# One decoder layer with paged latent attention on TensorE: the sample keys by token move from SyncE's DMA queue to GpSimd's

## The chip, the cores and the metric

The kernel is one program on one core of a Trainium2 chip. The metric is the time of one execution on the device in microseconds (us). The kernel before was run three times: 2036.37, 2043.57 and 2047.83 us, median 2043.57 us.

## What is computed

The reference is one layer of a decoder for two request groups with shared weights: a prompt of 256 tokens, and 8 sample sequences of 8 new tokens each, each behind 1024 cached tokens in 8 pages of 128. Only the part around the change is shown: the attention of one sample sequence over its cached latent (512 wide) and rotary key (64 wide), 16 heads.

```python
c_all = jnp.concatenate([cache_c[pages].reshape(n_past, KV_LORA), cn], axis=0)
kr_all = jnp.concatenate([cache_kr[pages].reshape(n_past, QK_ROPE), krn], axis=0)
q_lat = jnp.einsum('thd,rhd->thr', qn, w_uk)
s = (jnp.einsum('thr,lr->htl', q_lat, c_all) + jnp.einsum('thr,lr->htl', qr, kr_all)) * ATTN_SCALE
p = jax.nn.softmax(jnp.where(mask[None], s, -jnp.inf), axis=-1)
o_lat = jnp.einsum('htl,lr->thr', p, c_all)
return jnp.einsum('thr,rhd->thd', o_lat, w_uv)
```

The latent `c_all` is used twice: in the scores, where it has to lie with the latent index on the partitions ("by latent"), and in the sum over the tokens, where it has to lie with the token on the partitions ("by token").

## The kernel before, in words

All work is written out by hand on five engines, which meet only at semaphores. The weights come as slabs of 1 MB from DRAM into two buffers `w_raw`; ScalarE (ACT) rounds each to `w_hi` and VectorE (DVE) makes the rest `w_lo`, so that TensorE (PE) can multiply in three passes. The stages follow each other: input projections, gates, prompt attention (16 heads, with the products `ukt` for the sample queries between them), the sample stage, output projections, and a feed-forward part of 11 chunks that takes over half of the time. SyncE's queue (SP, SPq in the rows) issues nearly all transfers.

The sample stage is a loop over i = 0..8 in each engine, one sample sequence b per round, with two halves q of four pages each. `w_raw` and `c_raw` have one buffer for each half.

TensorE's round i (L1454 to L1489) is, in this order: `score(i, 0)`; the transposes of the probabilities of sequence i-1 (L1463, L1467); `score(i, 1)`; the scores of the new tokens; `values(i-1, 0)` and `values(i-1, 1)`, 32 matmuls each of `spt` with `c_raw`; and four matmuls with `cnew`. `score(i, q)` waits for `ql_lo_r >= i+1` (L1433), that is for `ql_lo` of sequence i. `values(b, q)` waits for `c_full[q]` (L1446) and raises `c_used` when it is done (L1452).

ScalarE's round i splits the pages of sequence i+1, makes `ql_hi` of sequence i+1 (`query_hi`, L632), and takes the exponentials. VectorE's round i makes `w_lo` of the pages, the maxima and the normed probabilities.

GpSimd (POOL) has one task in this stage: L421 to L424, a loop over b in which it waits for `ql_hi` of b and makes `ql_lo = qlat - ql_hi`.

SyncE loads both forms of the cache. `by_latent(b, q)` (L331) issues four transfers of 288 KB into `t_raw[q]`, which lies over `w_raw`; `by_token(b, q)` (L338) issues four of 256 KB into `c_raw[q]`. Both read the four page numbers from `page_sb` into registers first (`pages_of`, L316 to L320). `by_token(b, q)` waits for `values(b-1, q)` to be done (L341), and `by_token(0, 0)` for the last head of the prompt attention (L343), since `c_raw[0]` lies over buffers of that. In SyncE's loop (L357 to L371) `by_token(i, 0)` and `by_token(i, 1)` stand behind both `by_latent(i+2, q)`, and each of these behind a wait for the `w_lo` of the pages before them (L360); `by_token(0, 1)` stands ahead of the loop (L353).

Of the kernel before, what the change touches and what calls it, by code (L numbers as in the profile page):

```python
# [26 lines left out]
H, DN, DR, DV, R = 16, 128, 64, 128, 512  # L27
RT = R // P
PAST, PAGE = 1024, 128
NPG = PAST // PAGE  # L30
# [20 lines left out]
G0 = {}  # L51
# [6 lines left out]
QUAD = NPG // 2  # L58
# [4 lines left out]
def dense_index(g):  # L63

    return g if g < GS else g - 2 * NB
# [4 lines left out]
def split_index(g):  # L70

    return g - (4 if g > G0["ukt"] else 0) - (4 if g > G0["uv2"] else 0)
# [23 lines left out]
def program(nc, slabs, x, vecs, consts, cache_t, cache, pages, pool_hist, conv_hist,  # L96
            y, kv_out, kr_out, pool_out, conv_out):
    n_phys = cache.shape[0]
# [8 lines left out]
    def sb(name, shape, dt=F32, at=None):  # L107
        n = 4
        for d in shape[1:]:
            n *= d  # L110
        return nc.alloc_sbuf_tensor_at(name, shape, dt, offset=region(n) if at is None else at)

    with ExitStack() as ctx:
        def sem(name):
            return ctx.enter_context(nc.semaphore(name))
# [14 lines left out]
        page_sb = sb("page_sb", [1, NB * NPG], I32)  # L130
# [20 lines left out]
        c_raw = [sb("c_raw0", [P, QUAD * R], at=ch_reg), sb("c_raw1", [P, QUAD * R])]  # L151
# [63 lines left out]
        def const(name, n=None):  # L215
# [8 lines left out]
        vec_in, hist_in, again_in, chist_in = (sem(n) for n in ("vec_in", "hist_in", "again_in", "chist_in"))  # L224
# [3 lines left out]
        slab_used, slab_taken = sem("slab_used"), sem("slab_taken")  # L228
# [9 lines left out]
        sc_done, sc_masked, mx_done, ex_done, rc_done, pn_done, pt_done, pt_taken, pv_done, ohi_done, olo_done = (  # L238
            sem("p_" + n) for n in ("sc_done", "sc_masked", "mx_done", "ex_done", "rc_done", "pn_done", "pt_done",
                                    "pt_taken", "pv_done", "ohi_done", "olo_done"))  # L240
# [4 lines left out]
        c_full, c_used = [sem("c_full0"), sem("c_full1")], sem("c_used")  # L245
# [34 lines left out]
        @block.sync  # L280
        def _(sp):
            def x_part(c):

                sp.dma_start(xT[:, 4 * c:4 * c + 4, :], x[:, 4 * c:4 * c + 4, :]).then_inc(x_in[c], 16)

            def latent_rows(j, n0, n1):

                return (raw[j % 2][:, n0 * 4 * P:n1 * 4 * P].rearrange("p (n c) -> p n c", n=n1 - n0),
                        slabs[n0:n1, :, j * 4 * P:(j + 1) * 4 * P].rearrange("n p c -> p n c"))

            sp.dma_start(vec[:, :], vecs).then_inc(gain_in, 16)
            x_part(0)
            sp.dma_start(*latent_rows(0, 0, 2)).then_inc(slab0_half, 16)
            sp.dma_start(*latent_rows(0, 2, 4)).then_inc(raw_full[0], 16)
            x_part(1)
            sp.dma_start(*latent_rows(1, 0, 4)).then_inc(raw_full[1], 16)
            x_part(2)
            sp.wait_ge(lo_ready, 1)
            sp.dma_start(*latent_rows(2, 0, 4)).then_inc(raw_full[0], 16)
            x_part(3)  # L300
            sp.wait_ge(lo_ready, 2)
            sp.dma_start(*latent_rows(3, 0, 4)).then_inc(raw_full[1], 16)
            sp.dma_start(cst[:, :], consts).then_inc(vec_in, 16)
            sp.dma_start(page_sb[:, :], pages).then_inc(vec_in, 16)
            sp.dma_start(hist[:, :, :], pool_hist).then_inc(hist_in, 16)

            def stream(g0, g1):

                d0 = dense_index(g0)
                with sp.Fori(d0 // 2, (d0 + g1 - g0) // 2) as i:  # L310
                    for s in range(2):
                        sp.wait_ge(lo_ready, i * 2 + (split_index(g0) - d0 + s - 1))
                        sp.dma_start(raw[s], slabs[i * 2 + s]).then_inc(raw_full[s], 16)

            stream(RT, G0["ukt"])
            def pages_of(b, q):  # L316

                first = b * NPG + q * QUAD
                return nc.values_load_multi_w_load_instructions(  # L319
                    page_sb[0:1, first:first + QUAD], engines=(mybir.EngineType.SP,), min_val=0, max_val=n_phys - 1)[1]  # L320

            def whole_slabs(name, free):

                for q in range(2):
                    sp.wait_ge(slab_used, free + q + 1)
                    sp.dma_start(whole[2 + q], slabs[dense_index(G0[name] + 2 + q)]).then_inc(whole_full[q], 16)

            def into_raw(g):
                sp.dma_start(raw[g % 2], slabs[dense_index(g)]).then_inc(raw_full[g % 2], 16)

            def by_latent(b, q):  # L331

                pages4 = pages_of(b, q)
                for j in range(QUAD):
                    sp.dma_start(t_raw[q][:, j * TCOL:(j + 1) * TCOL],  # L335
                                 cache_t[bass.ds(pages4[j], 1)].rearrange("a p c -> (a p) c")).then_inc(t_full[q], 16)

            def by_token(b, q):  # L338

                if b:  # L340
                    sp.wait_ge(c_used, 2 * (b - 1) + q + 1)  # L341
                elif q == 0:
                    sp.wait_ge(pv_done, H)  # L343
                pages4 = pages_of(b, q)
                for j in range(QUAD):
                    sp.dma_start(c_raw[q][:, j * R:(j + 1) * R],  # L346
                                 cache[bass.ds(pages4[j], 1)].rearrange("a p c -> (a p) c")).then_inc(c_full[q], 16)

            for q in range(2):
                sp.wait_ge(lo_ready, G0["ukt"] + q - 1)  # L350
                into_raw(G0["ukt"] + q)
            whole_slabs("ukt", G0["ukt"] - 2)
            by_token(0, 1)  # L353
            for q in range(2):
                sp.wait_ge(slab_used, G0["ukt"] + q + 1)
                by_latent(0, q)
            for i in range(-1, NB):  # L357
                for q in range(2):
                    if i + 2 <= NB:
                        sp.wait_ge(lo_ready, split_index(GS + 2 * (i + 1) + q) + 1)  # L360
                    if i + 2 < NB:
                        by_latent(i + 2, q)
                    elif i + 2 == NB:
                        into_raw(G0["uv2"] + q)
                if i == NB - 1:
                    whole_slabs("uv2", G0["uv2"] - 2)
                if i == -1:
                    by_token(0, 0)
                if i >= 1:
                    for q in range(2):  # L370
                        by_token(i, q)  # L371
            for q in range(2):
                sp.wait_ge(slab_used, G0["uv2"] + q + 1)
                into_raw(G0["attn_out"] + q)
            stream(G0["attn_out"] + 2, NSLAB)
            sp.wait_ge(cs_done, 2 * FT)
            sp.dma_start(conv_out, cstate[:, :, :, :]).then_inc(out_sem, 16)
            for k in range(4):
                sp.wait_ge(y_step, 4 * (k + 1))
                sp.dma_start(y[:, 4 * k:4 * k + 4, :], x1[:, 4 * k:4 * k + 4, :]).then_inc(out_sem, 16)  # L380
            sp.wait_ge(st_done, 16)
            sp.wait_ge(out_sem, 16 * 7)
# [3 lines left out]
        def _(pool):  # L386
# [31 lines left out]
                last.then_inc(qrs_ready, 1)  # L418

            pool.wait_ge(qrs_ready, 4)  # L420
            for b in range(NB):  # L421
                pool.wait_ge(ql_hi_r, b + 1)
                nc.gpsimd.tensor_tensor(ql_lo[:, b % 2, :], qlat[:, b, :, :].rearrange("p j c -> p (j c)"),
                                        ql_hi[:, b % 2, :], ALU.subtract).then_inc(ql_lo_r, 1)  # L424

            pool.wait_ge(chist_in, 16)
            pool.wait_ge(slab_used, G0["ffn"])
# [1245 lines left out]
```

## Time and profile before

| what | value |
|---|---|
| median of three runs | 2043.57 us |
| time of the profiled execution | 2035.44 us |
| span of its trace | 2032.3 us |
| mean granted clock of TensorE | 0.989 |
| busy: TensorE / VectorE / ScalarE / GpSimd | 97% / 54% / 37% / 3% |
| busy in the sample stage, 716 to 839 us of the span (123 us): TensorE / VectorE / ScalarE / GpSimd | 113.96 / 53.74 / 51.95 / 6.33 us |
| DMA engines' mean busy share in that stretch | 0.75, 245 GB/s |

The span is the time from the first to the last instruction of the trace; the execution's own time is 3.1 us more. Busy time is that of instructions that compute: waits, register instructions and DMA issues are not in it. The clock is a share of TensorE's full speed. PEld is the loading of weights into TensorE, which lies beside its matmuls.

### The profile page before, as it was taken

The page shows a single profiled execution, that of the slowest core. Times are in us where ns is not written, and L with a number is a line of the kernel's source. Part 1 is how long each engine was busy: PE and PEld are TensorE (multiplying, and loading weights), DVE is VectorE, ACT ScalarE, POOL GpSimd, SP SyncE. Part 2 cuts the span into 40 slices and gives each one's busy share as a digit, 9 for nine tenths or more (in the row PEclk, how much of TensorE's full clock was granted, in tenths as well). Part 3 has the DMA queues.
Part 4 walks back from the last instruction along what each step waited for, and adds up shares of the span by engine and source line. Part 5 has one row for each costly group of instructions (what it writes and reads, how often), then busy time and mean ns, then how long its engine had stood idle before and what let it go on. Part 6 is the DMA issues. An engine that isn't in the chain of part 4 may idle for free.

```text
span 2032.3 us, 34080 instructions
## 1 busy us (share of the span) xinstructions
PE 1969.3 (97%) x13366; PEld 1942.9 (96%) x13366; DVE 1093.5 (54%) x1472; ACT 754.1 (37%) x813; POOL 54.4 (3%) x196
## 2 busy tenths in 40 slices
PE   8999999999999799999999999999999999999996
PEld 7999999999998688999999999999999999999996
DVE  6864344334345555255556555655556565565657
ACT  5456542332245554133334333333333333333332
POOL 0001000000000000000000000000000000000000
PEclk9999999999999899999999999999999999999998
DMA  6444444444453378544444434434444344443442
GB/s 243 145 145 161 153 145 147 158 150 145 144 186 111 114 248 267 204 162 150 145 146 151 164 140 152 147 142 165 142 147 148 143 164 144 144 152 141 161 145 101
DMA packets 59575, 318.14 MB, mean 157 GB/s; under 512 B 6466, under 2 KB 6658, under 8 KB 26882
## 3 DMA queue, kind: packets, MB, share of 16 engines
q1 hardware_dynamic: 58866, 313.15, 43.7%
q10 hardware_dynamic: 656, 4.27, 0.5%
q8 instruction: 34, 0.56, 0.1%
q14 instruction: 19, 0.16, 0.0%
HBM read 313.08 MB, written 4.32 MB: 156 GB/s over the span
## 4 chain that ended last, share of the span: by engine, by line
PE 90%; DVE 3%; ACT 3%; DMA 2%; issue 1%; SPq 1%; POOL 0%; DVEq 0%; ACTq 0%; POOLq 0%
PE ps L1199 90%; DVE w_lo L753 1%; ACT w_hi L457 1%; DMA c_raw<-in_cache 1%; DMA w_raw<-in_slabs 1%; DVE x L1192 0%; DVE k_rope L753 0%; ACT sm L639 0%; SPq L319 0%; SPq L335 0%; DMA xT<-in_x 0%; DVE neg_max L1029 0%; ACT k_rope L457 0%; SPq L346 0%; DMA w_raw<-in_cache_t 0%
## 5 line engine op out<-in xcount | busy, mean ns | idle before, releaser
L753 DVE TENSOR_TENSOR w_lo<-w_raw,w_hi 128x2048 fp32r<-128x2048 f32 (+1 forms) x267 | 609.7, 2284 | 459.8 <-ACT w_hi L457 459.6
L1199 PE MATMUL ps<-h_hi,w_hi 128*128 128x320 f32 x2512 | 742.2, 308 | 14.6 <-ACT w_hi L457 11.1
L457 ACT ACTIVATE w_hi<-w_raw 128x2048 fp32r<-128x2048 f32 (+1 forms) x267 | 508.3, 1905 | 639.6 <-PE ps L1199 632.8
L1199 PE MATMUL ps<-h_lo,w_hi 128*128 128x320 f32 x2512 | 741.1, 309 | 0.0
L1199 PEld LDWEIGHTS ps<-h_hi,w_hi 128*128 128x128 f32 x2512 | 473.3, 188 | 15.4 <-ACT w_hi L457 11.3
L1199 PEld LDWEIGHTS ps<-h_lo,w_hi 128*128 128x128 f32 x2512 | 471.5, 188 | 0.2
L1199 PE MATMUL ps<-h_hi,w_lo 128*128 128x320 f32 x2512 | 393.6, 308 | 0.0
L1199 PEld LDWEIGHTS ps<-h_hi,w_lo 128*128 128x128 f32 x2512 | 374.9, 187 | 0.0
L1199 PE MATMUL ps<-hid_hi,w_hi 128*128 128x320 f32 x704 | 216.7, 308 | 0.0
L1199 PE MATMUL ps<-hid_lo,w_hi 128*128 128x320 f32 x704 | 216.5, 308 | 0.0
L1199 PE MATMUL ps<-hid_hi,w_lo 128*128 128x320 f32 x704 | 216.5, 308 | 0.0
L1199 PEld LDWEIGHTS ps<-hid_hi,w_hi 128*128 128x128 f32 x704 | 131.9, 187 | 0.5 <-issue 0.3
L1199 PEld LDWEIGHTS ps<-hid_hi,w_lo 128*128 128x128 f32 x704 | 131.9, 187 | 0.0
L1199 PEld LDWEIGHTS ps<-hid_lo,w_hi 128*128 128x128 f32 x704 | 131.9, 187 | 0.0
L753 DVE TENSOR_TENSOR x<-ps,x 128x320 f32<-128x320 f32 x176 | 79.9, 485 | 46.5 <-PE ps L1199 46.4
L740 ACT ACTIVATE silu<-cv,vec 128x336 f32<-128x336 f32 x44 | 25.4, 577 | 213.2 <-DVE cv L1181 213.2
L1199 PE MATMUL ps<-o_hi,w_hi 128*128 128x320 f32 x256 | 75.5, 309 | 1.7 <-ACT w_hi L457 1.7
L1199 PE MATMUL ps<-m_hi,w_hi 128*128 128x320 f32 x256 | 75.3, 308 | 0.0
L1199 PE MATMUL ps<-o_lo,w_hi 128*128 128x320 f32 x256 | 75.3, 307 | 0.0
L1199 PE MATMUL ps<-m_lo,w_hi 128*128 128x320 f32 x256 | 75.3, 307 | 0.0
L1199 PE MATMUL ps<-spt,c_raw 128*128 128x128 f32 x512 | 62.3, 285 | 8.0 <-DMA c_raw<-in_cache 8.0
L1199 PEld LDWEIGHTS ps<-spt,c_raw 128*128 128x128 f32 x512 | 61.0, 201 | 8.5 <-issue 8.4
(212 smaller groups left out, 1749.0 us busy)
## 6 DMA issues: line engine op xcount, KB each, us to landing
w_raw<-in_slabs SPq DMA_DIRECT2D x253, 1024.0 KB, 4.8
w_raw<-in_cache_t SPq DMA_DIRECT2D x64, 288.0 KB, 3.6
c_raw<-in_cache SPq DMA_DIRECT2D x64, 256.0 KB, 3.7
w_whole<-in_slabs SPq DMA_DIRECT2D x4, 1024.0 KB, 6.5
xT<-in_x SPq DMA_DIRECT2D x4, 640.0 KB, 7.5
x_again<-in_x ACTq DMA_DIRECT2D x1, 2560.0 KB, 12.6
out_y<-x SPq DMA_DIRECT2D x4, 640.0 KB, 2.9
w_raw<-in_slabs SPq DMA_DIRECT2D x2, 512.0 KB, 6.1
```

Source lines behind the costliest of these rows:

```text
L457: return nc.scalar.activation(out, in_, ACT.Copy)
L740: nc.scalar.activation(silu[:, f % 2, CW - 1:], cv[:, 2, CW - 1:], ACT.Silu, bias=vec[:, bass.ds(c * FPC + (VEC["conv_b"] + f), 1)]).then_ ...
L753: return nc.vector.tensor_tensor(out, a, b, op)
L1199: return nc.tensor.matmul(out, a, b, start=start, stop=stop, **kw)
```

## The change

The transfers by token leave SyncE's program and are issued by GpSimd. `by_token` is defined there: it reads its four page numbers into GpSimd's registers, then waits, then issues four transfers. `by_token(0, 1)` and `by_token(0, 0)` stand ahead of GpSimd's loop over b, and `by_token(b, 0)` and `by_token(b, 1)` behind the `ql_lo` of b in that loop, for b = 1 to 7. The first waits for the slabs ahead of `ukt` to be used, in place of its old position in SyncE's order. The transfers, their sizes, their buffers and all other waits are the same.

```diff
@@ SyncE
-            def by_token(b, q):
-
-                if b:
-                    sp.wait_ge(c_used, 2 * (b - 1) + q + 1)
-                elif q == 0:
-                    sp.wait_ge(pv_done, H)
-                pages4 = pages_of(b, q)
-                for j in range(QUAD):
-                    sp.dma_start(c_raw[q][:, j * R:(j + 1) * R],
-                                 cache[bass.ds(pages4[j], 1)].rearrange("a p c -> (a p) c")).then_inc(c_full[q], 16)
-
...
-            by_token(0, 1)
...
-                if i == -1:
-                    by_token(0, 0)
-                if i >= 1:
-                    for q in range(2):
-                        by_token(i, q)
@@ GpSimd
             pool.wait_ge(qrs_ready, 4)
+            def by_token(b, q):
+
+                first = b * NPG + q * QUAD
+                pages4 = nc.values_load_multi_w_load_instructions(
+                    page_sb[0:1, first:first + QUAD], engines=(mybir.EngineType.Pool,), min_val=0, max_val=n_phys - 1)[1]
+                if b:
+                    pool.wait_ge(c_used, 2 * (b - 1) + q + 1)
+                elif q == 0:
+                    pool.wait_ge(pv_done, H)
+                else:
+                    pool.wait_ge(slab_used, G0["ukt"])
+                for j in range(QUAD):
+                    pool.dma_start(c_raw[q][:, j * R:(j + 1) * R],
+                                   cache[bass.ds(pages4[j], 1)].rearrange("a p c -> (a p) c")).then_inc(c_full[q], 16)
+
+            pool.wait_ge(vec_in, 32)
+            by_token(0, 1)
+            by_token(0, 0)
             for b in range(NB):
                 pool.wait_ge(ql_hi_r, b + 1)
                 nc.gpsimd.tensor_tensor(ql_lo[:, b % 2, :], qlat[:, b, :, :].rearrange("p j c -> p (j c)"),
                                         ql_hi[:, b % 2, :], ALU.subtract).then_inc(ql_lo_r, 1)
+                if b:
+                    for q in range(2):
+                        by_token(b, q)
```

## Rows read from the trace of the kernel before

**Rows 1.** The page: busy time of each engine, and the chain that ended last.

```profile
PE 1969.3 (97%) x13366; PEld 1942.9 (96%) x13366; DVE 1093.5 (54%) x1472; ACT 754.1 (37%) x813; POOL 54.4 (3%) x196
PE 90%; DVE 3%; ACT 3%; DMA 2%; issue 1%; SPq 1%; POOL 0%; DVEq 0%; ACTq 0%; POOLq 0%
```

**Rows 2.** Who waited for whom, TensorE, 600 to 860 us: total, times, longest.

```profile
PE ps L1199 <- DMA c_raw<-in_cache: 8.0, 4, 2.5
PE ps L1199 <- POOL ql_lo L423: 6.3, 2, 3.8
```

**Rows 3.** Timeline, rounds 3 and 4: start, duration, engine, what, [idle before it].

```profile
744.00 7.41 PE L1199 MATMUL ps<-spt,c_raw 128*128 128x128 f32 x64
...
745.69 0.62 ACT L457 ACTIVATE ql_hi<-qlat 128x512 fp32r<-128x512 f32 x1
...
746.38 1.26 POOL L423 TENSOR_TENSOR ql_lo<-qlat,ql_hi 128x512 fp32r<-128x512 f32 x1 [17.41 <-ACT ql_hi L457]
...
749.13 2.29 DVE L753 TENSOR_TENSOR w_lo<-w_raw,w_hi 128x2048 fp32r<-128x2048 f32 x1
...
751.25 1.06 PE L1199 MATMUL ps<-spt,cnew 128*128 128x128 f32 x8
...
751.73 0.79 DVE L1074 TENSOR_SCALAR s_probs<-s_probs,sample_sum 128x1088 f32<-128x1088 f32 x1
...
752.06 0.48 PE L1199 MATMUL ps<-w_hi,ql_hi 128*128 128x512 f32 x1
...
756.40 5.32 SPq L346 DMA_DIRECT2D c_raw<-in_cache  x8
...
762.46 7.38 PE L1199 MATMUL ps<-spt,c_raw 128*128 128x128 f32 x64 [1.57 <-DMA c_raw<-in_cache]
```

**Rows 4.** Timeline of TensorE: the other rounds that waited, and one that did not.

```profile
727.15 7.38 PE L1199 MATMUL ps<-spt,c_raw 128*128 128x128 f32 x64 [1.81 <-DMA c_raw<-in_cache]
...
798.00 8.97 PE L1199 MATMUL ps<-spt,c_raw 128*128 128x128 f32 x64 [2.06 <-DMA c_raw<-in_cache]
...
816.24 7.39 PE L1199 MATMUL ps<-spt,c_raw 128*128 128x128 f32 x64
...
828.03 9.01 PE L1199 MATMUL ps<-spt,c_raw 128*128 128x128 f32 x64 [2.52 <-DMA c_raw<-in_cache]
```

**Rows 5.** SyncE's issues: line L346 (min/median/max ns), its landing, timeline, chain.

```profile
L346 SPq DMA_DIRECT2D c_raw<-in_cache x56: 332/333/1560, 721.0 to 827.8; - x56
DMA to landing us min/median/max: 2.7/3.7/5.3
614.76 1.90 SPq L346 DMA_DIRECT2D c_raw<-in_cache  x4
716.09 0.30 SPq L319
...
717.60 0.33 SPq L335
```

**Rows 6.** Timelines of TensorE and GpSimd: from the prompt attention into the sample stage.

```profile
682.04 1.66 PE L1199 MATMUL ps<-pt,vv 128*128 128x256 f32 x8
684.78 1.26 POOL L423 TENSOR_TENSOR ql_lo<-qlat,ql_hi 128x512 fp32r<-128x512 f32 x1 [495.09 <-ACT ql_hi L457]
686.19 0.47 PE L1199 MATMUL ps<-w_hi,ql_hi 128*128 128x512 f32 x1 [2.49 <-POOL ql_lo L423]
689.07 0.39 PE L1199 MATMUL ps<-k_rope,q_rope_hi 128*128 128x512 f32 x1
```

**Rows 7.** The same passes one round later, and that stretch's granted clock (last but two).

```profile
697.75 0.77 PE L1199 MATMUL ps<-w_hi,ql_hi 128*128 128x512 f32 x1 [3.77 <-POOL ql_lo L423]
702.71 0.39 PE L1199 MATMUL ps<-k_rope,q_rope_hi 128*128 128x512 f32 x1
698.00:702.00 4.00, 4.00 (x10) 3.17 (x11) 3.86 (x6) 1.25 (x4) 0.00 (x0) 0.50 0.87 272
```

## The prediction

> **What bounds the kernel now.** I read the page first. TensorE is busy for 97% of the span and makes 90% of the chain that ended last; GpSimd is busy for 3% [rows 1]. So whatever makes TensorE stand still is paid in full, and an engine at 3% matters only where TensorE waits for it. Next I asked who waited for whom on TensorE in the sample stage. Two entries touch the change: four waits for the transfers into `c_raw`, 8.0 us together, and two for GpSimd's `ql_lo`, 6.3 us [rows 2]. The first is what the change can win; the second says that `ql_lo` is already on the path where it is late. Last I read the timeline of two rounds, for the order of events and the slack of each [rows 3].
>
> The round, with t = 0 where `values(b-1, 0)` starts (744.00): both halves of the values take 7.25, to 751.25, so one takes 3.6; `cnew` follows and the next `score(b+1, 0)` starts at 752.06, t = 8.1. `ql_hi` of b+1 is ready at t = 2.3 and `ql_lo` of b+1 runs from 2.4 to 3.6. The score that needs it starts at 8.1, so `ql_lo` now has 4.4 us of slack [rows 3]. SyncE issues the eight transfers by token only from 756.40, t = 12.4, though `c_raw` is free at 3.6 and 7.3: that is why TensorE waits 1.57 us at 762.46 [rows 3]. Rounds 2, 6 and 8 wait 1.81, 2.06 and 2.52 us [rows 4]. The rounds between them (3, 5, 7) don't wait.
>
> **The change part by part.** *What it removes.* SyncE loses 64 issues and 16 readings of page numbers. Its other transfers are named in neither entry of the waits [rows 2], so this alone is worth nothing: `by_latent` comes a little earlier, and what reads it waits for TensorE's scores anyway. The waits for `c_raw` of rounds 2, 4 and 6 go, 1.81 + 1.57 + 2.06 = 5.4 us. The wait of 2.06 was followed by values of 8.97 us where 7.39 is usual, so 1.6 us more go [rows 4]. Together **-7.0 us**.
>
> *What it adds to GpSimd.* Its order becomes: `ql_lo` of b; wait for `values(b-1, 0)`; four issues; four page numbers; wait for `values(b-1, 1)`; four issues; then `ql_lo` of b+1. That last one is queued behind two new waits and eight issues, and TensorE's `score(b+1, 0)` waits for it. The wait for `values(b-1, 1)` alone ends at t = 7.3, only 0.8 us before TensorE wants the `ql_lo` behind it, and `ql_lo` itself takes 1.26 us [rows 3]. So there is a stall in every round even if the issues cost nothing.
>
> *The price of an issue on GpSimd* is in no row. Below it is bounded by SyncE's own: 0.33 us each alone, and with register work between them four took 1.90 us, (1.90 - 0.33) / 3 = 0.52 us from one to the next. Above, by the longest issue of that line, 1.56 us [rows 5]. A gain from issuing is excluded, since the instructions are in the engine's order. I take the middle of 0.52 and 1.56, **1.04 us**: no row is GpSimd's own, and the rows give no side the better claim. Reading four page numbers takes 1.4 to 1.5 us on SyncE (716.09 to 717.60) [rows 5]; I use 1.4. [...]
>
> *The stall.* First issues from t = 3.8 to 3.8 + 4.16 = 8.0; page numbers to 9.4 (past the wait, which ended at 7.3); second issues to 13.5; `ql_lo` 1.26, with 0.07 ahead of it and 0.15 behind it [rows 3, 6], to 15.0. TensorE wanted to start at 8.1: **6.9 us, say 7.0**, in each round. It hits `ql_lo` of b+1 for b = 1 to 6, six times: **+42.0 us**. Nothing else on TensorE could be moved into it, as its order is fixed. GpSimd's first `ql_lo` stands behind `by_token(0, 0)`: the prompt attention ends at 683.7, four issues last to 688.0, and `ql_lo` starts at 688.1 in place of 684.78, where TensorE already waited for it [rows 6]: **+3.3 us**. `by_token(0, 1)` runs some 60 us earlier and costs nothing.
>
> *The clock.* [...] After 2.06 and 2.52 us it cost 1.6, after 1.57 and 1.81 nothing [rows 3, 4]. Stalls of 7 us lie beyond all of these: 6 x 2.1, and 2.1 for the first one, which grows from 2.49 to 5.8 us: **+14.7 us**.
>
> *The last round* has no score between, so the transfers for `values(7, q)` get little time. The values of round 7 start at 816.24; GpSimd may issue the first half at 820.0, done at 824.2, landed by the median of 3.7 us at 827.9; now it starts at 828.03. The second half is issued from 825.6 to 829.8 and lands at 833.5, 2 us after the first half is used up, while now the values also pay for the slow clock [rows 4, 5]. **0 us**, the one late wait that stays.
>
> *Elsewhere*: SyncE's queue keeps its order, the transfers carry the same 256 KB, and TensorE's rounds become longer, so the DMA engines have more time and not less.
>
> Sum: -7.0 + 42.0 + 3.3 + 14.7 + 0 = **+53.0 us**, 2088.4 us against the profiled execution's 2035.4. The median of the runs is 8.1 us above that execution; as a median I give 2043.6 + 53.0 = **2096.6 us**. A measurement of this kernel can tell about 0.5% (10 us) from no change.
>
> *The bounds.* At 0.52 us: the second issues run from 7.4 to 9.5, `ql_lo` ends at 11.0, a stall of 2.9, with 1.6 for the clock; six times 27.0, first `ql_lo` 1.2 + 2.1, waits -7.0, last round -3.8: +19.5 us. At 1.56 us: the stall is 11.1, six times 66.6, first `ql_lo` 5.4, clock 14.7, waits -7.0, last round +4.3: +84 us.
>
> **The rivals.**
> *A: the issues leave GpSimd at once (1 in 10).* If the queue takes them in no time, the stall is 7.4 + 1.5 - 8.1 = 0.8 us, six times 5 us, with no loss of clock, and the waits of all four rounds are won with both slow stretches, -8.0 - 3.2. That is -6 us, 2038 us as a median. Without any stall, had ScalarE's `ql_hi` been the later event, it would be -11 us, **faster** at 2032. The mechanism turns where the stall per round is below 11 / 6 = 1.9 us, that is at 0.27 us for an issue; SyncE's 0.33 speaks against that.
> *B: VectorE holds GpSimd up (15 in 100).* The issues from t = 3.8 to 13.5 fall on VectorE's `w_lo` of 2.29 us and the scaling of `s_probs` of 0.79 us [rows 3]. If GpSimd stands still for both, the stall grows by 3.1 us, six times 18.5, to +71.5 us, 2115 us. [...] Against B: `ql_lo` took 1.26 us in all rounds [rows 3, 6], but none of them ran beside a `w_lo`.
> *C: GpSimd reads its page numbers while issues are still in work (20 in 100).* Then the 1.4 us drop out, the stall is 5.5 us, and the sum +44 us: 2088 us.
> *D: cheap issues as on SyncE (10 in 100)*: +19.5 us, 2063 us.
> That the change does something else than it says is not to be expected: the two sides of the diff have the same 16 calls.
>
> **How the numbers follow.** Forecast 45 in 100, A 10, B 15, C 20, D 10. The range goes from the lower bound against the profiled execution, 2035.4 + 19.5 = 2055, to the upper against the median, 2043.6 + 84 = 2128, and leaves out A and what lies beyond the bounds. Slower by over 0.5%: forecast, B, C and nearly all of D, 0.89. Within 0.5%: most of A and a rest of D, 0.08. Faster: 0.03.
>
> **What would show it.** After the change TensorE's waits should name `ql_lo` 8 times, with some 7 us in six rounds and 50 us in all, and `c_raw` at most once or twice. The round should take 16.9 + 7.0 + 2.1 = 26 us. GpSimd's queue should show 64 issues of about 1 us, its `ql_lo` should start 13 to 14 us after the values in place of 2.4, and the granted clock should be below 1.00 at each start of a `score(b, 0)`. I am wrong if `ql_lo` still ends before `cnew`, or if the issues take under 0.4 us.

## The result, and the profile after

The changed kernel takes 2086.58 us (median of 4 runs, 2084.02 to 2087.68) against 2045.19 us before: ratio 1.0209, 95% interval 1.0174 to 1.0244. The forecast was 2096.6 us with a range of 2055 to 2128. It is slower by 41.4 us in the medians and by 52.1 us between the two profiled executions (2087.51 and 2035.44), whose spans differ by 53.5 us; the section on what was not expected says why these are not the same. Three executions far above all others of their kernels (3072.76, 3259.93 and 6323.46 us) are left out of every comparison below.

The page of the changed kernel, parts 1, 3 and 6:

```profile
span 2085.8 us, 34082 instructions
PE 1983.3 (95%) x13366; PEld 1952.5 (94%) x13366; DVE 1093.7 (52%) x1472; ACT 753.7 (36%) x813; POOL 92.4 (4%) x260
...
q0 software_dynamic: 5120, 16.78, 2.3%
...
c_raw<-in_cache POOLq DMA_DIRECT2D x64, 256.0 KB, 5.1
```

TensorE is 14.0 us longer busy with the same 13366 matmuls [rows 1]: the clock, granted at 0.977 in the mean in place of 0.989. GpSimd's busy time rises from 54.4 to 92.4 us. Of these 38.0 us the 64 issues are 34.8: the page counts them among GpSimd's instructions (260 in place of 196), while SyncE's issues are in no busy time. A transfer lands 5.1 us after its issue in place of 3.7 [rows 5].

Who waited for whom on TensorE, 600 to 920 us, answers to [rows 2]:

```profile
PE ps L1203 <- POOL ql_lo L424: 52.0, 8, 9.8
PE ps L1203 <- DMA c_raw<-in_cache: 1.8, 1, 1.8
```

The wait for `c_raw` has all but gone, 8.0 to 1.8 us, as the change meant it; the wait for `ql_lo` has come in its place, 6.3 to 52.0. These two entries and the busy time add up to the whole difference: 45.7 - 6.2 + 14.0 = 53.5 us.

The timeline of one round of the changed kernel, and TensorE's longest and shortest stall of the six:

```profile
769.36 7.39 PE L1203 MATMUL ps<-spt,c_raw 128*128 128x128 f32 x64
771.24 0.61 ACT L461 ACTIVATE ql_hi<-qlat 128x512 fp32r<-128x512 f32 x1
773.87 1.71 POOL L416 DMA_DIRECT2D c_raw<-in_cache  x3 [15.77 <-PE ps L1203]
775.82 0.54 POOL L416 DMA_DIRECT2D c_raw<-in_cache  x1 [0.25 <-issue]
776.59 1.06 PE L1203 MATMUL ps<-spt,cnew 128*128 128x128 f32 x8
777.74 1.71 POOL L416 DMA_DIRECT2D c_raw<-in_cache  x3 [1.38 <-PE ps L1203]
782.70 0.54 POOL L416 DMA_DIRECT2D c_raw<-in_cache  x1 [3.25 <-issue]
783.25 1.27 POOL L424 TENSOR_TENSOR ql_lo<-qlat,ql_hi 128x512 fp32r<-128x512 f32 x1
784.67 0.77 PE L1203 MATMUL ps<-w_hi,ql_hi 128*128 128x512 f32 x1 [7.02 <-POOL ql_lo L424]
...
733.37 0.77 PE L1203 MATMUL ps<-w_hi,ql_hi 128*128 128x512 f32 x1 [9.82 <-POOL ql_lo L424]
861.33 0.77 PE L1203 MATMUL ps<-w_hi,ql_hi 128*128 128x512 f32 x1 [5.28 <-POOL ql_lo L424]
```

`ql_hi` is ready 2.5 us after the start of the values, as before [rows 3], but `ql_lo` starts 13.9 us after it. In front of it stand both waits and all eight issues, and something that the forecast did not have: ahead of the eighth issue GpSimd stands still for 3.25 us, and the row names no engine that it waits for. Three issues take 1.71 us, so an issue takes 0.54 us and the next starts 0.58 us after it, not 1.04.

### The profile page after: what moved, and what is told of

Its sections match the earlier page's. It is cut to its first block, busy times and chain, and to the rows that moved or that the text cites. A ratio compares the mean times of both kernels' runs of the same rounds, so it can differ in the third digit from the quotient of the medians.

```text
span 2085.8 us, 34082 instructions
## 1 busy us (share of the span) xinstructions
PE 1983.3 (95%) x13366; PEld 1952.5 (94%) x13366; DVE 1093.7 (52%) x1472; ACT 753.7 (36%) x813; POOL 92.4 (4%) x260
## 4 chain that ended last, share of the span: by engine, by line
PE 90%; issue 3%; DVE 2%; ACT 2%; DMA 1%; POOL 1%; POOLq 0%; DVEq 0%; SPq 0%; ACTq 0%
PE ps L1203 89%; ACT w_hi L461 1%; DMA w_raw<-in_slabs 1%; DVE w_lo L757 1%; POOL ql_lo L424 0%; DVE x L1196 0%; POOL c_raw L416 0%; POOLq L407 0%; PE ps L1467 0%; ACT sm L643 0%; DMA c_raw<-in_cache 0%; DVE neg_max L1033 0%; DMA xT<-in_x 0%; DVE sm L1027 0%; ACT qlat L461 0%
## 5 line engine op out<-in xcount | busy, mean ns | idle before, releaser
L1203 PE MATMUL ps<-w_hi,ql_hi 128*128 128x512 f32 x64 | 34.4, 537 | 52.0 <-POOL ql_lo L424 52.0
L1203 PEld LDWEIGHTS ps<-w_hi,ql_hi 128*128 128x128 f32 x64 | 16.3, 254 | 56.6 <-issue 53.2
```

What stands on the lines that cost most here:

```text
L1203: return nc.tensor.matmul(out, a, b, start=start, stop=stop, **kw)
```

## The experiments

Every ratio is the time against the kernel before on the same chip, with its 95% interval. A ratio within half a per cent of 1 must be read with the two levels of time in the last section: how many executions fall at which level moves a median by as much. The first question was whether the loss is the place of `ql_lo` or GpSimd's queue; the second what the pause ahead of the last issue is.

**`ql_lo` ahead of the transfers.**

```diff
-            by_token(0, 0)
             for b in range(NB):
-                low_query(b)
+                if b + 1 < NB:
+                    low_query(b + 1)
                 if b:
                     for q in range(2):
                         by_token(b, q)
```

(`low_query(b)` is the wait for `ql_hi` and the subtraction; `low_query(0)` and then `by_token(0, 0)` stand ahead of the loop.)

> The transfers by token stay on GpSimd, but each ql_lo of b+1 is made ahead of by_token(b, 0) and (b, 1), and the first ql_lo ahead of by_token(0, 0). Theory (the cost is the place of ql_lo behind the issues and their waits, not the queue itself): all stalls on ql_lo fall back to the two of before (6.3 us), TensorE waits for c_raw at most once, in the last round (1.8 us), and the time is 6 to 11 us below the kernel before, ratio about 0.996. Rival (GpSimd's transfers themselves are late or disturb others): the waits for c_raw come back in most rounds and the time is at or above the kernel before.

Measured: 0.9966 (0.9939 to 0.9994). TensorE's waits for `ql_lo` are 6.6 us in place of 52.0. The queue is GpSimd's as in the changed kernel, and so are its transfers; the place of `ql_lo` alone undoes the loss. It gains nothing beyond that: the span of its profile is 2032.8 us, against 2032.3 for the kernel before at the same level of time. The waits for `c_raw` are five in four rounds, 5.7 us, and not one of 1.8, so the rival has a share. On this engine the eight issues are drawn out over the round by pauses up to 4.95 us ahead of the last one of a half.

**3072 and 512 bytes in place of 1024.** Both kernels set `dynamic_dma_scratch_size=1024`. One run had 3072, one 512. In the run with 3072 `kr_half`, which takes 2 x 256 x 4 = 2048 bytes of each partition, just the difference, was laid over `ql_hi` and is written a little later; a control has that move and 1024. The expectations call these bytes room for descriptors, and think of a pause as a wait for it. What lies in the bytes is seen in no trace. The traces show that GpSimd's time with nothing named is 86.9, 25.5 and 8.6 us at 512, 1024 and 3072 bytes.

```diff
-    nc = bacc.Bacc("TRN2", target_bir_lowering=False, num_devices=1, dynamic_dma_scratch_size=1024)
+    nc = bacc.Bacc("TRN2", target_bir_lowering=False, num_devices=1, dynamic_dma_scratch_size=3072)
-        kr_half = sb("kr_half", [P, 2, NP])
+        kr_half = sb("kr_half", [P, 2, NP], at=ol_reg + 16384)
```

> The changed kernel with 3072 bytes for each partition in place of 1024 for GpSimd's transfer descriptors; kr_half is moved over ql_hi to make room and is written a few us later. Theory (the fourth issue of the second half, which waits 1.3 to 4.1 us, waits for room that earlier transfers still hold): these gaps vanish, also the one of 6.2 us in round 2, each stall on ql_lo falls to 3.8 us, the six together from 43.5 to some 23 us, and the time is 20 us below the changed kernel, about 1.011 of the kernel before. [...]

> The changed kernel with kr_half over ql_hi as in the run with 3072 bytes, but the 1024 bytes for descriptors kept: the control of that run. If the room made its gain, this one is as slow as the changed kernel, 1.02 of the kernel before, with the gaps of 1.3 to 4 us ahead of the last issue. If moving kr_half made it, this one is at 1.012 too.

> The changed kernel with 512 bytes in place of 1024 for GpSimd's transfer descriptors. If room is what the late issues wait for: gaps ahead of the fourth issue of each half and of most of the second half, the second half done some 2 us later or more, and the time 10 to 30 us above the changed kernel (1.026 to 1.035 of the kernel before). Rival (no matter of room): the same time as the changed kernel, 1.021.

Measured: 3072 bytes 1.0125 (1.0089 to 1.0161); the control 1.0224 (1.0179 to 1.0269), so the move of `kr_half` gives nothing; 512 bytes 1.0489 (1.0447 to 1.0532), more than the 1.026 to 1.035 expected. The view of the tile `c_raw` on GpSimd says how long it stood ahead of its issues with nothing named, and how often: first 512 bytes, then 1024 (the changed kernel), then 3072.

```profile
  issue: 86.9, 37
```

```profile
  issue: 25.5, 15
```

```profile
  issue: 8.6, 4
```

Some of this is register work. In the changed kernel seven pauses of 1.25 to 6.24 us make 22.3 of the 25.5 us; with 3072 bytes three of 3.83, 0.61 and 2.81 us make 7.25 of the 8.6. TensorE's waits for `ql_lo` go with it: 93.2, 52.0 and 34.6 us. With 3072 bytes four of the six rounds look like the first three rows here, one has a pause of 0.61 us, and one the pause of 3.83 us, with the stall of the last row (timelines):

```profile
772.10 2.29 POOL L416 DMA_DIRECT2D c_raw<-in_cache  x4 [1.36 <-PE ps L1204]
774.41 1.27 POOL L424 TENSOR_TENSOR ql_lo<-qlat,ql_hi 128x512 fp32r<-128x512 f32 x1
775.83 0.77 PE L1204 MATMUL ps<-w_hi,ql_hi 128*128 128x512 f32 x1 [3.59 <-POOL ql_lo L424]
...
752.74 0.76 PE L1204 MATMUL ps<-w_hi,ql_hi 128*128 128x512 f32 x1 [7.87 <-POOL ql_lo L424]
```

So half of the six stalls is the order of the program (3.6 us a round, with the waits for the values, four issues and `ql_lo` itself: 21.6 of 43.5 us), and half (43.5 - 21.6 = 21.9 us) goes with the pauses in the middle of GpSimd's issues, 21.1 us of them in these six rounds. With the two pauses that are left in the six rounds, the run with 3072 bytes keeps 26.3 us of the 43.5.

The pauses go by the count of issues. With 3072 bytes they come ahead of GpSimd's 22nd, 42nd and 62nd issue, 20 apart, and in the run below that issues one half alone, with 1024 bytes, ahead of its 8th, 15th and 22nd, 7 apart: a third of the bytes, about a third of the count. In the changed kernel they come ahead of the 12th, 24th, 32nd, 40th, 48th, 56th and 64th.

**The waits alone.** All transfers stay on SyncE; GpSimd gets the waits of the changed kernel in their places.

```diff
+            pool.wait_ge(pv_done, H)
             for b in range(NB):
                 ...
+                if b:
+                    for q in range(2):
+                        pool.wait_ge(c_used, 2 * (b - 1) + q + 1)
```

> The kernel before, with all transfers on SyncE, but GpSimd has the waits of the changed kernel in the places they have there: pv_done ahead of its loop and both c_used behind each ql_lo. It has no issue and no page number. Theory (the waits alone cost only what lies between the end of the values and the wanted ql_lo): ql_lo ends 0.7 us after TensorE wants it in six rounds, 4.5 us in all, and part of it is taken back from the waits for c_raw: 1.000 to 1.002 of the kernel before. Rival (the waits alone make the loss): some 1.02.

Measured: 0.9971 (0.9947 to 0.9995). The six stalls on `ql_lo` are there and as small as expected, from this timeline 0.65 to 0.67 us each, and 1.9 us come back from `c_raw` (6.1 us in place of 8.0):

```profile
755.75 0.47 PE L1203 MATMUL ps<-w_hi,ql_hi 128*128 128x512 f32 x1 [0.67 <-POOL ql_lo L424]
...
774.43 0.47 PE L1203 MATMUL ps<-w_hi,ql_hi 128*128 128x512 f32 x1 [0.65 <-POOL ql_lo L424]
```

The waits are not the loss. That the ratio is below 1 is no gain of theirs: at equal level of time this run is within 1 us of the kernel before (last section).

**Only the first half on GpSimd.** Its loop keeps `by_token(b, 0)`; SyncE issues the second half in the old place.

```diff
                 if b:
-                    for q in range(2):
-                        by_token(b, q)
+                    by_token(b, 0)
```

> Only the transfers of the first half go from GpSimd, the second half from SyncE as before. Theory (what stalls TensorE is the second half, whose wait ends 0.8 us before TensorE wants the ql_lo behind it): four issues of 0.58 us from t = 4.5 end at 6.8, ql_lo ends at 8.2 where TensorE wants it at 8.1, so the six stalls are 0.2 us each and cost no clock; the waits for c_raw go, since SyncE has four issues less ahead of the second half. Time 3 to 9 us below the kernel before, 0.996 to 1.000. Rival (any issue ahead of ql_lo costs its own share): half the loss, 1.010.

Measured: 1.0084 (1.0049 to 1.0119), so the expectation was wrong and the rival's number right, but not the rival's reason. Timelines of GpSimd and TensorE:

```profile
742.02 2.29 POOL L427 DMA_DIRECT2D c_raw<-in_cache  x4 [14.66 <-PE ps L1212]
744.33 2.12 POOL L434 TENSOR_TENSOR ql_lo<-qlat,ql_hi 128x512 fp32r<-128x512 f32 x1
746.59 0.47 PE L1212 MATMUL ps<-w_hi,ql_hi 128*128 128x512 f32 x1 [0.79 <-POOL ql_lo L434]
...
759.69 1.13 POOL L427 DMA_DIRECT2D c_raw<-in_cache  x2 [13.24 <-PE ps L1212]
767.17 1.15 POOL L427 DMA_DIRECT2D c_raw<-in_cache  x2 [6.35 <-issue]
768.34 1.27 POOL L434 TENSOR_TENSOR ql_lo<-qlat,ql_hi 128x512 fp32r<-128x512 f32 x1
769.76 0.76 PE L1212 MATMUL ps<-w_hi,ql_hi 128*128 128x512 f32 x1 [6.26 <-POOL ql_lo L434]
```

Where four issues go through, the stall is 0.6 to 0.8 us and not 0.2, since `ql_lo` beside VectorE's `w_lo` takes 1.95 to 2.12 us in place of 1.26 (rival B, below). In every second round a pause of 4.1 to 6.9 us falls among the issues, and the stall is 4.3 to 6.8 us. So with 1024 bytes even four issues ahead of `ql_lo` are too many. The pause is also there though the group before its own had been issued 15 to 18 us earlier: from 742.02, against 759.69. As no transfer of this run lands later than 7.3 us after its issue, it is no wait for that group to land. What ends a pause stays open. The pauses end 4.7 to 8.6 us after the first issue of their own four here (7.5 in the rows shown) and 3.0 to 8.0 in the changed kernel, about where the landings lie (3.0 to 7.3 us from the issue here, 2.8 to 7.6 there). But one pause of the run with 3072 bytes ends 1.2 us after the first issue of its four (810.85 to 812.01), sooner than any transfer of that run lands (2.9 us).

**The same gain without GpSimd.** If TensorE waited for `c_raw` only because its issues stood behind the second `by_latent`, a change of order on SyncE should do.

```diff
                 for q in range(2):
+                    if q and i >= 1:
+                        for half in range(2):
+                            by_token(i, half)
                     if i + 2 <= NB:
                         sp.wait_ge(lo_ready, split_index(GS + 2 * (i + 1) + q) + 1)
...
-                if i >= 1:
-                    for q in range(2):
-                        by_token(i, q)
```

That is the second of two such orders ("both between"). The first ("each behind its own") had `by_token(i, q)` right behind `by_latent(i+2, q)` and was run twice.

> The kernel before, all on SyncE, but by_token(i, q) stands right behind by_latent(i+2, q) in place of behind both. Theory (TensorE waited for c_raw only because both halves were queued behind the second by_latent): the first half is issued from t = 7, five us earlier, the waits for c_raw fall from 8.0 us to at most 2, and the time is 6 to 10 us below the kernel before, 0.995 to 0.998. Rival (the second by_latent, now four issues later, makes TensorE wait for its pages): 1.000 or above, with waits for w_hi or w_raw.

> The order on SyncE with by_token(i, q) right behind by_latent(i+2, q), once more beside the one above: 0.996 to 0.999 of the kernel before; waits for c_raw of 5.6 us in all.

> The kernel before, all on SyncE, but both by_token(i, q) stand between by_latent(i+2, 0) and by_latent(i+2, 1). If the remaining waits for c_raw of the run with the changed order on SyncE (the second half, 0.5 to 1.3 us) come from its place behind the second by_latent, they go, and TensorE waits for c_raw in the last round alone, some 3 us; time 6 to 10 us below the kernel before, 0.995 to 0.997. Rival (the second by_latent, now behind a wait for the values and four more issues, is late): waits for w_hi take their place, 1.000 or above.

Measured: each behind its own 0.9986 (0.9959 to 1.0013) and 0.9951 (0.9925 to 0.9976), with waits for `c_raw` of 5.6 and 5.2 us and not the 2 expected; the second half is still late, by 0.4 to 1.3 us. Both between: 0.9948 (0.9925 to 0.9972). Its waits for `c_raw` are 2.0 us, in the last round; waits for `ql_lo` grow to 10.4, with 1.19, 0.86 and 2.12 us in three rounds, because the second `by_latent` is now late: ScalarE waits for it for 25.5 us in all (0.6 before), and its `ql_hi` comes behind. So the rival holds in part. Both orders beat both kernels with every transfer on SyncE, but by less than the last ratios say. Of the 11 runs of the second order 2 were at the upper level of time, of the 22 of the kernel before beside them 15. At equal level "both between" is 5 us faster than the kernel before, and "each behind its own" 5 to 9 (table in the last section), so the second order is not shown to be better than the first.

**`ql_lo` ahead, with 3072 bytes.** The edit is the first one and the one to 3072 bytes together.

> ql_lo ahead of the transfers, as in the first run, with 3072 bytes for descriptors. Theory (that run's remaining waits for c_raw, 5.7 us, come from issues that waited for room, 0.7 to 4.9 us ahead of the last one of a round): they fall to 2 us or less and the time is 3 us or more below that run, about 0.994 of the kernel before. Rival (transfers from GpSimd simply land later than SyncE's): the waits stay at some 5 us, 0.997.

Measured: 1.0005 (0.9977 to 1.0032). The waits for `c_raw` are 4.2 us against 5.7, a fall, but not to 2; the ratio says nothing within its interval. The pauses come ahead of the 22nd, 42nd and 62nd issue here too (3.56, 0.61 and 0.62 us). The rival holds a part: the transfers land 4.7 us after their issue.

**The kernel before, profiled again**, twice, for the two levels told below.

> The kernel before, unchanged, for a second profile of it. Its executions lie at two levels, 2032 to 2040 and 2045 to 2052 us; the profile shown of it is of the lower one. Theory (the upper level is a fall of TensorE's clock in the uv2 products right behind the sample stage, as in the profile of the waits alone, where the products with ola took 421 ns in place of 275): if this execution is at the upper level, its products with ola take 421 ns and the granted clock is 0.5 there; if at the lower one, 275 ns. Rival (the levels have another cause): no such tie.

> The same as the run before it, for a third profile: an upper-level time goes with products with ola of 421 ns, a lower-level time with 275 ns.

Both fell at the lower level (2036.88 and 2037.97 us) with products with `ola` of 275 ns; the upper level of this very kernel has no profile.

## Why the prediction was right, step by step

| term | forecast, us | by the trace, us |
|---|---|---|
| waits for `c_raw` | -5.4 | -6.2 |
| six stalls on `ql_lo` | +42.0 | 9.82 + 6.58 + 7.02 + 7.82 + 6.96 + 5.28 = +43.5 |
| first `ql_lo` | +3.3 | 4.70 - 2.49 = +2.2 |
| clock, with the stretch of slow values that goes | 14.7 - 1.6 = +13.1 | 1983.3 - 1969.3 = +14.0 |
| sum | +53.0 | +53.5 |

**The mechanism** was right: `ql_lo` queued behind waits and issues. It is shown by the run that only moves `ql_lo` (52.0 us of waits become 6.6). The rounds take 24.4 to 28.1 us from values to values, around the 26 forecast.

**The size of the stalls was right for a wrong reason.** The price of an issue, "the middle of 0.52 and 1.56, 1.04 us", failed: the rows after show 0.54 busy and 0.58 from one to the next, hardly more than the 0.52 on SyncE. The 7 us of a round are 3.6 by order and price (the run with 3072 bytes) and 1.7 to 6.2 from the pauses, which no term had. Two errors met: a price too high by 0.46 us for up to eight issues, and pauses of up to 6.24 us that were not foreseen. That they cancel is luck. Rival D, cheap issues, had the right price, and its 2.9 us a round is near the 3.6 measured without a pause. With it the sum would have been +19.5 and far too low.

Part of the 3.6 is a delay that was not counted: from the end of the values to the first issue pass 1.1 us (776.6 to 777.74), with register work and about 0.5 us in which the row names nothing. The forecast had 0.1 to 0.2.

**The page numbers** were priced right at 1.4 us, but in most rounds they hardly count: with cheap issues they are read by 777.1, half a microsecond after the second wait has ended. Only in the round with the pause of 6.24 us, where that wait was long over, they stand in the way whole (1.40 us). Rival C holds to the extent that the first read starts beside the last issue (775.80 against 775.82); what it could save is the half microsecond.

**The clock** behaved as taken from the rows of before. The 2.1 us for each stall are worked out from two of them: the same 12 passes take 702.71 - 697.75 = 4.96 us in the stretch with a granted clock of 0.50, behind the stall of 3.77 us [rows 7], and 689.07 - 686.19 = 2.88 us at 1.00, behind the one of 2.49 [rows 6]. After the stall of 6.58 us, in the changed kernel's windows (the last but two is the granted clock):

```profile
758.00:763.00 5.00, 4.76 (x11) 3.80 (x12) 0.00 (x0) 0.00 (x0) 0.10 (x1) 0.50 0.65 244
763.00:768.00 5.00, 5.00 (x26) 4.16 (x25) 0.69 (x1) 2.70 (x5) 0.00 (x0) 0.92 0.00 0
```

The granted clock is 0.50 for 3 to 5 us behind each of the six stalls (the 5 us from the end of each have a mean of 0.50 to 0.70), and TensorE is busy for 14.0 us more in all. In the run with the waits alone the stalls of 0.65 and 0.67 us shown above were followed by passes of 0.47 us at a granted clock of 1.00.

**Rival A** (issues for nothing) fell with the 0.54 us and the pauses. **Rival B** (VectorE holds GpSimd up) did not decide the time, but the traces show it at a smaller size. Timelines of GpSimd and VectorE, from the run with `ql_lo` ahead and, in the second fence, from the one with the first half:

```profile
753.37 0.91 POOL L416 DMA_DIRECT2D c_raw<-in_cache  x1 [0.25 <-issue]
753.37 0.79 DVE L1084 TENSOR_SCALAR s_probs<-s_probs,sample_sum 128x1088 f32<-128x1088 f32 x1
...
768.01 3.27 DVE L763 TENSOR_TENSOR w_lo<-w_raw,w_hi 128x2048 fp32r<-128x2048 f32 x1
```

```profile
743.03 2.29 DVE L766 TENSOR_TENSOR w_lo<-w_raw,w_hi 128x2048 fp32r<-128x2048 f32 x1
```

An issue beside VectorE's scaling of `s_probs` takes 0.91 us in place of 0.54; issues beside `w_lo` keep their 0.54. `ql_lo` beside `w_lo` takes 2.12 us in place of 1.26, or `w_lo` takes 3.27 in place of 2.29. GpSimd does not stand still for the whole of a scaling, as rival B had it: the issue grows by 0.37 us beside one of 0.79. By what means the one delays the other is seen in no trace. In the changed kernel the delay is worth next to nothing: no issue there is longer than 0.68 us, and every `ql_lo` takes 1.26 to 1.27. Where only the first half is on GpSimd, the 0.7 to 0.9 us more that `ql_lo` takes account for the stalls of 0.6 to 0.8 us.

**The last round** was put at zero and cost 1.83 us of wait in place of 2.52.

## What to carry to other kernels

An idle engine is a good place for a transfer only if nothing behind it in its program is on the path: look for what is queued behind the new wait, and when that is wanted. Here 4.4 us of slack turned into 7 us of stall each round, and each stall cost 2 us more through the clock. First try the order within the queue that has the transfers: what was to be had, 5 to 9 us, lay there.

## What was not expected

**GpSimd stops in the middle of its issues.** In the changed kernel, with 1024 bytes, GpSimd stops for up to 6.24 us in the middle of its issues, and no row names a releaser. Its time ahead of issues with nothing named was 86.9, 25.5 and 8.6 us at 512, 1024 and 3072 bytes, and the pauses come at regular counts of issues. The kernel before has the same 1024 bytes, and no transfer of it is issued by GpSimd. Once GpSimd issued 64, the time was 1.0489, 1.0209 and 1.0125 of the kernel before at 512, 1024 and 3072 bytes, so the number has to be looked at together with such a change.

**One kernel, two levels of time.** Executions of the kernel before lie at 2032 to 2040 and at 2043 to 2052 us, and those of most variants too lie at two levels some 10 us apart. Four profiles are of executions at the upper level (the waits alone, 3072 bytes, both between, each behind its own again): in all four the products with `ola` right behind the sample stage take 421 ns. Seven are at the lower level (the kernel before three times, `ql_lo` ahead with 1024 and with 3072 bytes, the first half, each behind its own): 275 ns in all seven. The control with 1024 bytes spreads from 2081 to 2090 us for another reason: its profiled execution was the slowest of four and had 275. From the run of the waits alone, 2048.84 us, its tile `ola` and its windows:

```profile
L1203 PE MATMUL ps<-ola,w_whole x64: 421/421/421, 852.5 to 865.9; 128*128 128x64 f32 x64
```

```profile
853.00:866.00 13.00, 13.00 (x63) 13.00 (x62) 3.14 (x3) 2.30 (x3) 0.00 (x0) 0.50 0.25 88
```

TensorE is busy without a gap there, with matmuls of 64 columns, and the clock still goes to 0.50. One kernel has a profile at each level, "each behind its own": 2030.25 us with 275 ns and 2040.96 us with 421 ns, and TensorE busy for 1968.0 and 1980.4 us, 12.4 us more. This is what lies between the 53.5 us of the two traces and the 41.4 of the medians: the profile of before is of the lower level, 2035.44, and most runs behind its median of 2045.19 are of the upper, while the changed kernel's profile shows 275 ns and its four runs lie within 3.7 us. The forecast put the sum on the median and so came out 10 us high. That the upper level of the kernel before itself is this fall of the clock is argued from the other kernels, and not shown by a profile of it; what puts an execution at one level or the other is not known.

The levels also carry most of the small ratios. Medians of each level, in us, with the difference from the kernel before at the same level and beside it (lower: mean granted clock of 0.987 and more):

| kernel | lower | upper | executions at the upper level |
|---|---|---|---|
| before, three batches | 2036.7, 2035.5, 2037.3 | 2048.8, 2049.3, 2048.2 | 16 of 23, 8 of 23, 15 of 22 |
| `ql_lo` ahead | 2034.5 (-2.2) | 2049.2 (+0.4) | 3 of 12 |
| the waits alone | 2035.8 (-0.9) | 2048.3 (-0.4) | 4 of 12 |
| `ql_lo` ahead, 3072 bytes | 2033.7 (-1.7) | 2045.8 (-3.5) | 6 of 12 |
| each behind its own | 2030.1 (-5.4) | 2042.1 (-7.3) | 7 of 11 |
| each behind its own, again | 2028.3 (-9.0) | 2040.8 (-7.4) | 6 of 11 |
| both between | 2031.9 (-5.5) | 2043.6 (-4.6) | 2 of 11 |

The first two batches of the kernel before ran on the same chip, and 16 and then 8 of 23 executions were at the upper level. So the share moves without any edit, and a median over both levels moves with it.
